# Two of the four C groups of a state-space layer computed between the last two turns of its convolution loop

## The reference, cut to what matters

```python
zxbcdt = h @ w_in                       # for the context (256 tokens) and for the latent (256)
xbc = silu(dwconv1d(zxbcdt[..., D_INNER:D_INNER + SSD_CONV_DIM], conv_w, conv_b))   # 5 taps over time
xs = xbc[..., :D_INNER]                 # 2048 channels: 16 columns of 128
Bm = xbc[..., D_INNER:D_INNER + SSD_GN] # 1024 channels:  8 columns
Cm = xbc[..., D_INNER + SSD_GN:]        # 1024 channels:  8 columns, wanted for the latent only
...
states = einsum("bcsgn,bcsgj,bcsgjp->bcgjpn", Bc, decay_to_end, x)   # of the context
y = ssd(latent, initial state = the context's)
```

## Time and profile before

| what | value |
|---|---|
| median of 3 runs | 2096.06 us (2094.34 to 2097.07) |
| profiled execution | 2096.1 us, span of the profile 2094.4 us |
| TensorE busy | 1922.6 us (92%) |
| GpSimd busy | 1256.4 us (60%) |
| VectorE busy | 1045.1 us (50%) |
| ScalarE busy | 996.5 us (48%) |
| convolution loop's last SiLU to the first matmul of the heads | about 1316 to 1358 us of the span |

### The profile page before, as it was taken

The page is one execution under the profiler, slowest core; times in us unless marked ns, Lnnn a source line. Parts: engine busy times, 40 slices in busy tenths (PEclk is TensorE's granted clock), DMA queues, the critical chain, the costliest instruction groups (busy, mean ns, idle before and its releaser), DMA issues.

```text
span 2094.4 us, 33918 instructions
## 1 busy us (share of the span) xinstructions
PE 1922.6 (92%) x13589; PEld 1698.0 (81%) x13589; DVE 1045.1 (50%) x1512; ACT 996.5 (48%) x1722; POOL 1256.4 (60%) x588
## 2 busy tenths in 40 slices
PE   6989989998999989989999899898879997978997
PEld 6879788886999866868887788866669987938996
DVE  4473336633510173146666655688665623845631
ACT  3653435543444373435543444388645536325542
POOL 8667556687788504546678334200569885326885
PEclk9999999999999999999999999999989998989999
DMA  6335367774555404357763212221235553224552
GB/s 254 141 133 190 114 228 306 298 278 160 183 182 188 154 1 174 148 210 294 306 258 141 81 64 98 81 80 61 101 122 189 186 192 121 105 81 151 186 192 103
DMA packets 48321, 342.30 MB, mean 163 GB/s; under 512 B 5264, under 2 KB 6288, under 8 KB 7248
## 3 DMA queue, kind: packets, MB, share of 16 engines
q1 hardware_dynamic: 45968, 328.22, 42.7%
q0 software_dynamic: 2240, 12.49, 1.5%
HBM read 339.65 MB, written 1.05 MB: 163 GB/s over the span
## 4 chain that ended last, share of the span: by engine, by line
PE 64%; DVE 16%; ACT 7%; POOL 5%; issue 5%; DMA 2%; DVEq 0%; SPq 0%; POOLq 0%; ACTq 0%
PE bank L1734 12%; PE bank L1679 11%; PE bank L1683 11%; PE bank L1681 11%; DVE arena L917 2%; POOL w_hi L2188 2%; PE bank L1784 2%; PE bank L1292 2%; PE bank L1294 2%; PE bank L1295 2%; PE bank L1714 2%; PE bank L1713 2%; PE bank L1711 2%; POOL w_lo L2188 2%; DMA ring<-slabs_dram 2%
## 5 line engine op out<-in xcount | busy, mean ns | idle before, releaser
L2188 POOL TENSOR_TENSOR w_lo<-ring,w_hi 128x1024 fp32r<-128x1024 f32 x360 | 874.3, 2455 | 297.1 <-ACT w_hi L2769 296.8
L1679 PE MATMUL bank<-x_hi,w_hi 128*128 128x256 f32 x2176 | 616.5, 283 | 26.8 <-POOL w_lo L2188 16.6
L1683 PE MATMUL bank<-x_lo,w_hi 128*128 128x256 f32 x2176 | 618.8, 284 | 0.0
L2769 ACT ACTIVATE w_hi<-ring 128x1024 fp32r<-128x1024 f32 x448 | 448.9, 1052 | 344.6 <-DMA ring<-slabs_dram 337.2
L1679 PEld LDWEIGHTS bank<-x_hi,w_hi 128*128 128x128 f32 x2176 | 414.9, 191 | 47.3 <-issue 46.1
L1683 PEld LDWEIGHTS bank<-x_lo,w_hi 128*128 128x128 f32 x2176 | 414.3, 190 | 0.0
L1681 PE MATMUL bank<-x_hi,w_lo 128*128 128x256 f32 x1472 | 413.4, 281 | 0.0
L1681 PEld LDWEIGHTS bank<-x_hi,w_lo 128*128 128x128 f32 x1472 | 281.3, 191 | 0.0
L2188 POOL TENSOR_TENSOR w_hi<-ring,w_hi 128x1024 fp32r<-128x1024 f32 x88 | 209.0, 2398 | 111.8 <-ACT w_hi L2769 111.8
L2693 ACT ACTIVATE arena<-bank 128x512 f32<-128x512 f32 (+1 forms) x182 | 100.1, 563 | 291.0 <-PE bank L1683 191.8
L1681 PE MATMUL bank<-x_hi,w_hi 128*128 128x256 f32 x704 | 198.1, 281 | 0.0
(11 more groups left out here) (350 smaller groups left out, 3516.0 us busy)
## 6 DMA issues: line engine op xcount, KB each, us to landing
ring<-slabs_dram SPq DMA_DIRECT2D x308, 1024.0 KB, 4.8
lnrow<-ln_dram POOLq DMA_DIRECT2D x6, 1024.0 KB, 5.0
arena<-slabs_dram SPq DMA_DIRECT2D x4, 1024.0 KB, 7.8
xt<-xT_dram SPq DMA_DIRECT2D x1, 1024.0 KB, 6.0
xt<-memT_dram POOLq DMA_DIRECT2D x1, 1024.0 KB, 14.1
x<-x_dram POOLq DMA_DIRECT2D x1, 1024.0 KB, 18.0
arena<-ctx_dram POOLq DMA_DIRECT2D x1, 1024.0 KB, 6.1
lnrow<-ln_dram POOLq DMA_DIRECT2D x2, 512.0 KB, 4.8
```

The lines of the kernel that those rows point to most:

```text
L1679: ins = pe.matmul(dst, wh[:, k, c], src[0][:, k, :], start=(k == 0), stop=False)
L1683: ins = pe.matmul(dst, wh[:, k, c], src[1][:, k, :], start=False, stop=(k == KC - 1))
L2188: pool.tensor_tensor(dst[:, c], ring[:, s, c], w_hi[:, s, c].bitcast(F32), ALU.subtract).then_inc(S["lo_ready"], 1)
L2769: a.activation(w_hi[:, g % RING, c], ring[:, g % RING, c], ACT.Copy) \
```

## The change

`columns_of_c(j)` is the body of the loop over the C groups, made a function. Groups 0 and 1 are issued at the head of the convolution loop's turns 24 and 25, each ahead of that turn's transposes; groups 2 and 3 stay behind the loop. Only TensorE's list changes.

```diff
+            def columns_of_c(j):
+
+                pe.wait_ge(free_of(j), frees(j))
+                for c in range(2):
+                    ins = half(24 + 2 * j + c, bank[j][:, c * T:(c + 1) * T], *lat, True)
+                fill(ins, j, "act", "dve")
+
             for j in range(24 + 2):
+                if j >= 24:
+                    columns_of_c(j - 24)
                 if j == 1:
                     time_steps(7, lat)
                 if j < 24:
...
             marks["xs"] = mark("act")
-            for j in range(4):
-                pe.wait_ge(free_of(j), frees(j))
-                for c in range(2):
-                    ins = half(24 + 2 * j + c, bank[j][:, c * T:(c + 1) * T], *lat, True)
-                fill(ins, j, "act", "dve")
+            columns_of_c(2)
+            columns_of_c(3)
```

## The result

| | before | after |
|---|---|---|
| median | 2096.88 us (7 runs, 2094.34 to 2101.14) | 2106.26 us (7 runs, 2103.88 to 2106.82) |
| ratio of the times | | 1.0039, interval 1.0029 to 1.0049 |
| profiled execution, span | 2096.06, 2094.4 us | 2104.94, 2103.2 us |

The change makes the kernel slower by 8.2 us (1.0039 of 2096; 6.1 to 10.3 by the interval; the medians differ by 9.4). Forecast were 2105.9 us and a profiled execution 9.8 us longer; it is 8.9 longer.

A forecast was written before the change was run, and what follows sets the result against it. The stretch was taken as bound by the ScalarE-VectorE tap chain, not TensorE. Terms: + 9.3 (state inputs uncovered 5.3, held behind GpSimd 4.0) + 0.5 (slow clock, group 3) = + 9.8 on 2096.1: 2105.9 us, range 2100.4 to 2108.8.

The forecast's parts named there:

- Pair 23 starts at 1324.1, 11.94 us after the first: TensorE, convolution loop's end: last transpose pair starts at 1324.1, not 1316.83, behind C groups 0 and 1.
- State inputs uncovered, 5.3: VectorE: the four groups' state inputs, formerly covered by C group 0, delay group 0's taps by 5.3 us.
- Held behind GpSimd, 4.0: VectorE's state inputs collide with GpSimd's subtractions of halves 28 and 29: 4.0 us more before group 0's taps.
- its price, 0.7: If GpSimd starts before VectorE's third state input is issued, four inputs instead of three run behind it: 0.7 us more.
- Group 2 waits 5 us, hidden: TensorE idles 5 us for half 28 before C group 2, which still ends before it is wanted at 1339.6.
- Group 3 waits 7 to 8 us, cost 0.5: TensorE idles 7 to 8 us for half 30 before C group 3; slow clock after it costs 0.5 us.
- States 0 to 3 not in the way: TensorE's state matmuls 0 to 3 (6.9 us) end at 1358.5, ahead of the fifth's input at 1359.7.
- Rival 4: Slow clock lasts through C group 3 or falls again on states 4 to 7: 3 us more, 2109; chance 0.07.
- Nothing given back downstream: Behind the stage everything moves along, slab loads waiting for TensorE's progress; no time is given back.
- Rival 1: VectorE's state inputs aren't held by GpSimd: + 5.3 us, group 3's clock hidden or nearly, 2101.5; chance 0.12.
- Rival 2: TensorE is the bound; ScalarE and VectorE catch up, so the change gains 6.1 us: 2090.0; chance 0.05.
- Rival 3: No change: the loss is waited out further on, at a slab load not yet landed; 2096; chance 0.05.

The follow-up runs named there:

- Experiment 2: The change, but ScalarE converts halves 28 and 29 in turn 24 into two other buffers; median 2102.95 us, + 5.2 us against the kernel before.
- Experiment 3: The change, but VectorE computes the state inputs of group j behind the taps of C group j; median 2100.68 us, + 3.8 us against before.
- experiment 5: The kernel before plus three unused GpSimd subtractions of 128x1024, which read SBUF, beside the state inputs; median 2102.33 us, + 6.3 us.
- kernel 6: The kernel before plus seven GpSimd MEMSETs of 128x1024, which only write SBUF, beside the state inputs; median 2096.40 us, - 0.2 us.
- experiment 1: The kernel before with only C group 0 moved ahead of transposes 22 and 23, group 1 behind the loop; median 2102.49 us, + 5.4 us.
- experiment 9: Experiment 8's kernel plus three unused float32 matmuls between the state matmuls of groups 1 and 4; median 2092.59 us, - 3.4 us against before.
- experiment 4: Against before: only C group 0 moved, state inputs of group j behind the taps of C group j; median 2096.45 us, - 1.0 us.
- experiment 7: Experiment 1's kernel plus 32 matmuls, later overwritten, on TensorE between C groups 2 and 3; median 2101.27 us, + 4.4 us against before.
- experiment 8: Against before: C group 0 moved; state inputs 2, 3 in VectorE's gap, 0, 1 behind taps; state matmuls 2, 3 first; median 2094.89 us, - 1.5 us.

## Why the prediction was right, point by point

- *Pair 23 starts at 1324.1, 11.94 us after the first.* Measured 1313.44 to 1325.38: 11.94. The idle time and the slow clock in group 0 are gone, and worth nothing, as VectorE waits for this pair.
- *State inputs uncovered, 5.3.* Experiment 2 shows this alone: 5.17. They began 0.93 us after the pair, 0.99 was taken. Experiment 3 adds that a second thing stood behind the pair, ScalarE's copy and first tap: the forecast has it in its terms, but by itself it costs only 0.26.
- *Held behind GpSimd, 4.0.* 9.26 less 5.17 is 4.1. The count was right too: three free, the fourth and fifth held, three free. It hung on 0.35 us, the lead of the third input over GpSimd; the prediction gives its price, 0.7. GpSimd was forecast for 1326.95, which is 0.1 less than the terms named for it add up to (1325.0 and 2.05); measured, less the 1.28 by which the stage began later, it is 1326.83. Experiments 5 and 6 show that GpSimd's reading subtractions hold VectorE, and its MEMSETs don't. The inputs ended 22.73 us after the stage's start; forecast, by the pace of the earlier trace rows, were 22.7. By the rule of the Trainium skill that the prediction cites, taken strictly, the term would have been 10.1, and the measurement, which decides, is 0.8 less: GpSimd's two took 5.33 together, so VectorE's part lies mostly inside GpSimd's 2.67 and is not added to it.
- *Group 2 waits 5 us, hidden.* The gap was 5.04 us, the clock behind it 0.50, and ScalarE didn't wait for the group.
- *Group 3 waits 7 to 8 us, cost 0.5.* The gap was 6.71, somewhat short because group 2 ended late at its slow clock; the cost was 0.48 (first tap at 1352.94; the earlier turns, 5.79 us apart, would have put it at 1352.46). The size of this term was a near thing: in experiments 1 and 2 the same cause gave 1.4 and 1.2.
- *States 0 to 3 not in the way; the clock not low behind them.* The row of state group 4 shows a gap of 1.09 us, and from it to the heads it is 8.17 us in both kernels. Rival 4 is out.
- *Nothing given back downstream.* In the profiled executions 11.0 us of shift at the heads (9.75 and the 1.28 by which the stage began later, behind identical code) became 8.9 at the end. That is no more than profiles of the same code differ by: from the heads to the end of the span it is 736.4 us before and 734.1 after, and 734.3 to 737.1 in the nine other kernels, whose code is the same there; kernel 6, whose stage is as long as before, has 734.3. Such differences are there ahead of the stage too: the transposes that stand at 1198.11 in the earlier trace rows start at 1200.08 in the profile after.
- *The rivals.* Rival 1 (not held) fell with the 2.73 and 2.77 us; experiment 2 is what it would have been, 2102.95 at a forecast of 2101.5, with 1.16 us of it for group 3, which that forecast took as nearly hidden. Rival 2 (TensorE the bound) fell with VectorE's 8.69 us of waiting. It is right about one thing, though: with VectorE's order changed as well and a gap filled, a kernel with group 0 moved gains 3.4 us (experiment 9). Rival 3 fell with the result.

## What to carry to other kernels

An idle gap on the busiest engine isn't an offer until it is known what waits behind the instruction that ends the gap: here 4 us of idle time on TensorE covered nothing, and filling it took the cover from 5.8 us of VectorE work, which stood in a fixed order ahead of the taps. To fill such a gap, change the consumers' order in the same edit (put on VectorE first what doesn't need the delayed result, and the rest behind the critical taps), and look where the next gap and GpSimd's next reads fall: a gap cost time anew in experiments 1 to 4, 7 and 8, GpSimd's reads in 1, 3 to 5 and 8.

## What the runs showed of the hardware

- Delay makes more delay: in experiment 5 three added GpSimd reads cost the state inputs 5.0 us, and the delayed inputs met the next two reads and lost 4.2 more.
- The clock fell to 0.50 within a few microseconds behind short pauses of 2.06, 2.09, 2.90 and 3.44 us (experiments 7, 3, 8 and 4), not behind the 1.09 us of the changed kernel or the 1.17 us of the kernel before at the same place. Ahead of all of these TensorE was at work on state matmuls. Behind a pause of 0.35 us it stayed up too (experiment 9).
- Filling one pause with unused matmuls helped where it was the last one ahead of the stage's end (9: 1.8 us of the stage) and not where another pause followed (7: none).
- VectorE's taps, which read one tensor from PSUM and one from SBUF, aren't held: eight take 4.11 us beside GpSimd's subtractions and 4.11 us when it is idle (the earlier trace rows and the taps at 1354.07 above).
